# Feed-forward, first product: six 256-column products a block pair in two PSUM banks, instead of 512- and 256-column products in four

## The reference, cut to what matters

```
def squared_relu_mlp(h, w1, w2):
    return jnp.square(jax.nn.relu(h @ w1)) @ w2      # w1: 2048 x 8192, w2: 8192 x 2048

x = x + squared_relu_mlp(rms_norm(x, norm_ffn_g[l]), w_ff1[l], w_ff2[l])
```

## Time and profile before

| | us |
|---|---|
| median of 3 runs | 1606.09 (1605.94 to 1606.55) |
| span of the profiled execution | 1604.8 |
| TensorE busy in it | 1595.9 |
| VectorE busy | 1252.5 |
| ScalarE busy | 866.1 |
| FF1 of groups 1, 2, 3, each | 89.16, 89.17, 89.17 |
| FF2 of groups 1, 2 | 84.33, 84.97 |

### The profile page before, as it was taken

The page is one execution under the profiler, slowest core; times in us unless marked ns, Lnnn a source line. Parts: engine busy times, 40 slices in busy tenths (PEclk is TensorE's granted clock), DMA queues, the critical chain, the costliest instruction groups (busy, mean ns, idle before and its releaser), DMA issues.

```text
span 1604.8 us, 22691 instructions
## 1 busy us (share of the span) xinstructions
PE 1595.9 (99%) x7962; PEld 1352.9 (84%) x7962; DVE 1252.5 (78%) x1681; ACT 866.1 (54%) x1120; POOL 75.9 (5%) x160
## 2 busy tenths in 40 slices
PE   9999999999999999999999999999999999999998
PEld 8888888888888888888888888888888888888886
DVE  5588889999989898786887665885677666866587
ACT  7444456555555556754566655454464455545555
POOL 6500010000000000000000000000000000000001
PEclk9999999999999999999999999999999999999999
DMA  7665645555555665556664566666666666666555
GB/s 256 203 192 184 196 151 171 177 176 174 184 171 170 210 207 181 200 183 238 210 197 138 164 186 191 201 198 190 190 211 196 182 185 196 197 197 187 192 187 182
DMA packets 161294, 304.97 MB, mean 190 GB/s; under 512 B 11689, under 2 KB 20513, under 8 KB 160801
## 3 DMA queue, kind: packets, MB, share of 16 engines
q1 hardware_dynamic: 160128, 300.45, 58.9%
q0 software_dynamic: 1056, 3.46, 0.6%
q10 hardware_dynamic: 32, 0.01, 0.0%
HBM read 301.78 MB, written 2.10 MB: 189 GB/s over the span
## 4 chain that ended last, share of the span: by engine, by line
PE 98%; DVE 1%; DMA 1%; issue 0%; ACT 0%; SPq 0%; ACTq 0%; POOL 0%; DVEq 0%; POOLq 0%
PE ps L2255 15%; PE ps L1750 12%; PE ps L1752 12%; PE ps L1751 12%; PE ps L2025 9%; PE ps L2024 9%; PE ps L2023 9%; PE ps L2257 7%; PE ps L1763 1%; PE ps L1929 1%; PE ps L2146 1%; PE ps L1932 1%; PE ps L1914 1%; PE ps L1913 1%; PE ps L1912 1%; DMA raw<-in_w_ff_dram 1%
## 5 line engine op out<-in xcount | busy, mean ns | idle before, releaser
L1079 DVE TENSOR_TENSOR w_both<-raw,w_both 128x1024 fp32r<-128x1024 f32 x538 | 656.6, 1223 | 257.0 <-ACT w_both L624 255.3
L624 ACT ACTIVATE w_both<-raw 128x1024 fp32r<-128x1024 f32 x538 | 568.7, 1060 | 527.7 <-PE ps L1752 181.7
L2255 PE MATMUL ps<-a_both,w_both 128*128 128x512 f32 x1024 | 321.9, 396 | 0.0
L1750 PE MATMUL ps<-w_both,a_both 128*128 128x512 f32 x636 | 252.4, 397 | 0.1
L1752 PE MATMUL ps<-w_both,a_both 128*128 128x512 f32 x636 | 248.3, 390 | 0.0
L1751 PE MATMUL ps<-w_both,a_both 128*128 128x512 f32 x636 | 248.2, 390 | 0.0
L2257 PEld LDWEIGHTS ps<-a_both,w_both 128*128 128x128 f32 x1024 | 192.5, 188 | 45.2
L1140 DVE SCALAR_TENSOR_TENSOR acc<-hconv,cwk,acc 128x256 f32<-128x256 f32 x464 | 205.1, 497 | 7.4 <-PE ps L1968 7.4
L2257 PE MATMUL ps<-a_both,w_both 128*128 128x256 f32 x1024 | 201.4, 278 | 0.0
L2023 PE MATMUL ps<-w_both,c_hi 128*128 128x512 f32 x504 | 196.7, 390 | 0.3 <-DVE w_both L1079 0.3
L2025 PE MATMUL ps<-w_both,c_lo 128*128 128x512 f32 x504 | 196.4, 390 | 0.0
(11 more groups left out here) (377 smaller groups left out, 1920.3 us busy)
## 6 DMA issues: line engine op xcount, KB each, us to landing
raw<-in_w_ff_dram SPq DMA_DIRECT2D x256, 512.0 KB, 4.1
raw<-in_w_in_dram SPq DMA_DIRECT2D x144, 512.0 KB, 3.6
raw<-in_w_mla_out_dram SPq DMA_DIRECT2D x32, 512.0 KB, 3.7
raw<-in_w_conv_out_dram SPq DMA_DIRECT2D x32, 512.0 KB, 4.3
raw<-in_w_out_dram SPq DMA_DIRECT2D x32, 512.0 KB, 4.5
raw<-in_w_ukv_dram SPq DMA_DIRECT2D x16, 512.0 KB, 3.8
raw<-in_w_xkv_dram SPq DMA_DIRECT2D x16, 512.0 KB, 4.0
raw<-in_w_uq_dram SPq DMA_DIRECT2D x16, 384.0 KB, 3.3
```

What stands on the lines that cost most here:

```text
L624: act.activation(whi[:, s, :], raw[:, s, :], ACT.Copy).then_inc(hi_ready, 1)
L1079: dve.tensor_tensor(wlo[:, s, :], raw[:, s, :], whi[:, s, :].bitcast(F32), ALU.subtract).then_inc(lo_ready, 1)
L1750: pe.matmul(sum_, x_hi[:, k0 + k, tok], w_hi, start=(first and k == 0), stop=False)
L2255: pe.matmul(both, whi[:, s, cols[n]], a_both[:, :, k0 + k, :], start=(first and k == 0), stop=False)
```

## The change

In FF1 every bank now holds two blocks of 128 hidden columns, 256 tokens each, so that a chunk takes two banks (0 and 1, or 4 and 5) in place of four. A block's three products (`whi` x `a_hi`, `whi` x `a_lo`, `wlo` x `a_hi`), each of 256 columns, accumulate in the same columns. `ff_take` and `ff_add` are gone with `ff_low` and `ff_sum`; `ff_relus` reads the two banks directly and waits for `used` itself, and it now stands ahead of the `lo` of its step. TensorE waits for `ff_relu` where it waited for `ff_sum`.

```diff
         def ff1_banks(c):
-            return slice(CPB * (c % 2), CPB * (c % 2 + 1))
+            return slice(CPB * (c % 2), CPB * (c % 2) + 2)
...
-            def ff_take(n):
-                c = n % CH
-                act.activation(ff_row[:, c % 2, :, :], ps[:, ff1_banks(c), SEQ:], ACT.Copy).then_inc(ff_low, 1)
...
-                    act.wait_ge(used, r + (U_FF + UPC * (c + 1)))
-                    if c >= 2:
-                        act.wait_ge(ff_lo, g * CH + (c - 1))
-                    if c == 2:
-                        act.wait_ge(h_made, g * 4 + 12)
-                    ff_take(c)
...
-            def ff_add(c, done):
-                dve.wait_ge(ff_low, done)
-                row = ff_row[:, c % 2, :, :]
-                dve.tensor_tensor(row, ps[:, ff1_banks(c), 0:SEQ], row, ALU.add).then_inc(ff_sum, 1)
-            def ff_relus(c, done):
-                dve.wait_ge(ff_sum, done)
+            def ff_relus(c, units, done):
+                dve.wait_ge(used, units)
+                wait(dve, ff_lo, done - 2)
                 row = ff_row[:, c % 2, :, :]
+                sums = ps[:, ff1_banks(c), :].rearrange("p b (k s) -> p (b k) s", k=2)
                 by = rs_row[:].rearrange("p (k s) -> p k s", k=1).to_broadcast([P, CPB, SEQ])
-                dve.scalar_tensor_tensor(out=row, in0=row, scalar=0.0, in1=by, op0=ALU.max, op1=ALU.mult).then_inc(ff_relu, 1)
+                dve.scalar_tensor_tensor(out=row, in0=sums, scalar=0.0, in1=by, op0=ALU.max, op1=ALU.mult).then_inc(ff_relu, 1)
...
+                        if first and c == 1 and k == 0:
+                            dve.wait_ge(rs_row_ready, 1)
                         if c and k == 0:
-                            ff_add(c - 1, g * CH + c)
+                            ff_relus(c - 1, r + (U_FF + UPC * c), g * CH + c)
...
-                        if c and k == 0:
-                            ff_relus(c - 1, g * CH + c)
...
                 for k in range(2):
-                    for b in range(0, CPB, 2):
-                        cols = [slice(NC * k + P * n, NC * k + P * (n + 1)) for n in (b, b + 1)]
-                        for n in range(2):
-                            both = ps[:, b0 + b + n, :].rearrange("p (h s) -> p h s", h=2)
-                            pe.matmul(both, whi[:, s, cols[n]], a_both[:, :, k0 + k, :], start=(first and k == 0), stop=False)
-                        for n in range(2):
-                            mm = pe.matmul(ps[:, b0 + b + n, 0:SEQ], wlo[:, s, cols[n]], a_hi[:, k0 + k, :], start=False, stop=(last and k == 1))
+                    for half in range(2):
+                        blocks = [(ps[:, b0 + n, SEQ * half:SEQ * (half + 1)], slice(NC * k + P * (2 * n + half), NC * k + P * (2 * n + half + 1)))
+                                  for n in range(2)]
+                        for to, cols in blocks:
+                            pe.matmul(to, whi[:, s, cols], a_hi[:, k0 + k, :], start=(first and k == 0 and half == 0), stop=False, skip_group_check=True)
+                        for to, cols in blocks:
+                            pe.matmul(to, whi[:, s, cols], a_lo[:, k0 + k, :], start=False, stop=False, skip_group_check=True)
+                        for to, cols in blocks:
+                            mm = pe.matmul(to, wlo[:, s, cols], a_hi[:, k0 + k, :], start=False, stop=(last and k == 1 and half == 1), skip_group_check=True)
```

More of the change, by code:

```diff
@@ L383, in build @@
         rs_spread, rs_turned, rs_row_ready = (sem(n) for n in ("rs_spread", "rs_turned", "rs_row_ready"))
-        ff_low, ff_sum, ff_relu, ff_square, ff_hi, ff_lo = (sem(n) for n in ("ff_low", "ff_sum", "ff_relu", "ff_square", "ff_hi", "ff_lo"))
+        ff_relu, ff_square, ff_hi, ff_lo = (sem(n) for n in ("ff_relu", "ff_square", "ff_hi", "ff_lo"))
         h_lifted, h_made, h_hi_ready, h_lo_ready = (sem(n) for n in ("h_lifted", "h_made", "h_hi_ready", "h_lo_ready"))
@@ L1665, in ff_group @@
                             last_diag.then_inc(rs_spread, 1)
-                        if first and c == 1 and k == 0:
-                            dve.wait_ge(rs_row_ready, 1)
-                        if c and k == 0:
-                            ff_relus(c - 1, g * CH + c)
                         if c and k == 2:
@@ L1677, in ff_group @@
                         if p == 0 and k == 0:
-                            ff_add(CH - 1, g * CH + CH)
+                            ff_relus(CH - 1, r + (U_FF + UPC * CH), g * CH + CH)
                         i = k + LEAD
@@ L1685, in ff_group @@
                             lo(U_FF + u + i, r)
-                        if p == 0 and k == 0:
-                            ff_relus(CH - 1, g * CH + CH)
                         if p == 0 and k == 3:
@@ L2268, in ff_group @@
                     else:
-                        pe.wait_ge(ff_sum, g * CH + (c - 1))
+                        pe.wait_ge(ff_relu, g * CH + (c - 1))
                     for k in range(UPC):
@@ L2281, in ff_group @@
                             mm.then_inc(rs_turned, 1)
-                pe.wait_ge(ff_sum, g * CH + (CH - 1))
+                pe.wait_ge(ff_relu, g * CH + (CH - 1))
                 def ff_waits(i, k):
@@ L2286, in ff_waits @@
                     if i == LEFT[0]:
-                        pe.wait_ge(ff_sum, g * CH + CH)
+                        pe.wait_ge(ff_relu, g * CH + CH)
                 def mixed_waits(i, k):
```

## The result

| | before | after |
|---|---|---|
| median of 4 runs, us | 1606.01 (1605.94 to 1606.55) | 1618.54 (1618.43 to 1619.33) |
| ratio, 95% interval | | 1.0078 [1.0065, 1.0090] |
| span of the profiled execution | 1604.8 | 1616.7 |
| TensorE busy, products | 1595.9, 7962 | 1608.1, 8986 |
| VectorE, ScalarE busy | 1252.5, 866.1 | 1236.4, 851.9 |

What follows compares the result with a forecast made beforehand. The prediction took TensorE's products to bound the kernel: +12.0 for FF1's short products, +0.1 backlog and -0.6 for the gap gave +11.5 us, so 1606.1 + 11.5 = 1617.6 us, range 1606 to 1620.

Steps and rivals of the forecast that it cites:

- TensorE is the path, the rest lies beside it: Whole kernel: TensorE, busy 1595.9 of 1604.8 us, sets the end; ScalarE and VectorE work counts only where TensorE waits.
- A round costs 0.720 us for 0.6966, +12.0 us: FF1: six 256-column products at 0.120 us replace a round of four; 512 rounds at +0.0234 us each give +12.0 us.
- Rival 3: FF1: supplying 768 products unbroken costs another 1 to 2 ns each, 1621 to 1624 us; chance 0.05, shared with another rival.
- The reason given for it: FF1: the 128-column weight load, no longer hidden under a 512-column neighbour, sets an unbroken train's pace at 120 ns.
- the sign would turn: FF1: at 116.1 ns a product (696.6 / 6) the change would turn from slower to faster.
- The page's rule: FF1: the skill's load of 107 ns for 128 columns hides under a 256-column product; round 680 ns, sum -8.5 us.
- rival 1: FF1: loads hide under 256-column products and the round falls to 680 ns, -8.5 - 0.6, 1597.0 us; chance 0.08.
- The backlog: End of each FF1 stretch: two or three products late by 5 to 10 ns, 0.1 us in all.
- The ramp from PSUM: Behind each FF1 chunk: the ramp takes 1.22 to 1.23 us from PSUM, `lo` ends a microsecond earlier; cost nothing.
- The busy times forecast: Copy and add removed from FF1: 16.5 us less busy on ScalarE, 19.7 on VectorE; DVE near 1233, ACT near 850.
- The gap: FF2: 0.60 us lost behind two late transfers; everything from the first `lo` on comes 1.0 us earlier, so -0.6 us.
- The sum: Whole kernel: +12.0 + 0.1 - 0.6 = +11.5 us, span 1616.3, median 1617.6 us.

Runs made afterwards that it cites:

- e_no_add: Kernel before with its own products but no copy and add; the ramp leaves the high-weights, low-tokens product out of the sum: 1606.31 us, ratio 1.0000.
- e_tok240: Changed kernel with 240 of 256 tokens moving in FF1's products, all 128 weight columns loaded: 1593.62 us.
- e_tok128: Changed kernel with 128 of 256 tokens moving in FF1, all 128 weight columns loaded: 1593.36 us; the same with 224 tokens: 1592.80 us.
- e_cols64: Changed kernel with only 64 of each block's 128 weight columns loaded in FF1, 256 tokens still moving: 1602.35 us.
- e_tok192: Changed kernel with 192 of 256 tokens moving in FF1, all 128 weight columns loaded: 1593.15 us.
- e_alternate: Kernel before with an FF1 round's products by turns, 512, 256, 512, 256 columns in place of 512, 512, 256, 256: 1609.78 us, ratio 1.0022.
- e_fours: Kernel before with two FF1 rounds drawn together, four products of 512 columns, then four of 256: 1608.69 us, ratio 1.0015.
- e_cols96: Changed kernel with 96 of each block's 128 weight columns loaded in FF1, 256 tokens still moving: 1606.31 us.

## Why the prediction was right, point by point

- **TensorE is the path, the rest lies beside it.** Right. After the change no wait of TensorE behind the kernel's start is left in the list of waits, and without the element work alone the time stays where it was (e_no_add: 1606.31 beside 1606.22).
- **A round costs 0.720 us for 0.6966, +12.0 us.** Right: 92.16 a stretch was forecast and measured. The number came from rows of the same shape, not from a price for a load and one for columns. That is what made it hold. Rival 3, the supply of the train, fell: 768 products in a row keep the pace of 36, and e_tok240 sends as many 0.1117 apart, so the supply doesn't set 0.120.
- **The reason given for it** (the 128-column load sets the pace at 120 ns) was only half right. The floor that I take for the load's pace is 111.6 ns (e_tok128, 192, 224, 240) and the columns alone 113.3 (e_cols64 in groups 1 to 3); 120 is what the two give together. Both lie under 116.1, the point where the sign would turn, so a sum from separate prices would have said faster. The sentence that misled is "The forms differ in the weight load, which takes 192 ns for 128 columns and 135 for 64": a length in a row is no pace (192 ns loads start 111.6 apart in e_tok192). Nor was it safe to read from the key that a 64-column load gives 113.3: e_cols64 holds 120 with such loads for 600 products. And more than the load differs between the two rows, the moving operand too. The runs bear out that the load's size counts in FF1; the two rows alone did not show it.
- **The page's rule.** The Trainium skill gives 107 ns for such a load ("TensorE: Matmul & The Clock Gate", "LDWEIGHTS (loading the stationary operand)"), near the floor of 111.6 measured here. What the case contradicts is the step from there to "hidden": rival 1 would have come at 1597.0.
- **The backlog, +0.1 us.** Too small to see: the FF2 stretches behind a train are 84.34, before 84.33.
- **The ramp from PSUM costs nothing.** Right. The timeline of TensorE and VectorE behind the first chunk's end (926.63), answering to the earlier trace rows:

```profile
926.39 0.40 PE L2240 MATMUL ps<-a_both,w_both 128*128 128x256 f32 x2
926.63 0.40 PE L2236 MATMUL ps<-a_both,w_both 128*128 128x256 f32 x2
...
926.90 1.23 DVE L1625 SCALAR_TENSOR_TENSOR ff_row<-ps,rs_row 128x1024 f32<-128x1024 f32 x1 [1.02 <-PE ps L2240]
928.05 1.22 DVE L1068 TENSOR_TENSOR w_both<-raw,w_both 128x1024 fp32r<-128x1024 f32 x1
```

  The ramp takes 1.23 us; the `lo` ends at 929.27, 2.6 us behind the chunk's end, where it was 3.6 and 2.7 was forecast. The busy times forecast were too low: VectorE lost 16.1 us and not 19.7, ScalarE 14.2 and not 16.5. Rows overlap (the add's 1.23 us start 1.15 ahead of the next row), so a removed row takes less than its length off the busy time. Nothing on the path hangs on it.
- **The gap goes, -0.6 us.** It went (84.97 to 84.34), but the reason given isn't borne out, and here the forecast had luck. The copy and the add gone, the chain a microsecond earlier, a gap of 0.48 us stayed in e_no_add, with a transfer of 6.60 us in its chain as one of 6.72 in the earlier trace rows. And with the copy and the add still there it was gone in e_alternate (and in e_fours, 84.37). That the slower FF1 gives the transfers more time doesn't explain it either: in e_cols96 FF1 takes 89.1 as before, in e_cols64 87.05, and there is no gap (e_tok128, at 85.7, has a small one, 84.60). FF2 of group 2 in e_cols96, then in e_alternate:

```profile
1339.67:1424.01 84.34, 84.34 (x375) 69.80 (x373) 67.41 (x63) 43.34 (x46) 0.00 (x0) 1.00 0.62 206
1341.85:1426.19 84.34, 84.34 (x374) 69.85 (x373) 68.45 (x64) 44.26 (x47) 0.00 (x0) 1.00 0.63 205
```

  Each trace is one execution. A transfer that happens to be late in one and not in another would fit all of these (the prediction's own "a slow transfer can fall elsewhere"); it isn't shown.
- **The sum.** +11.5 forecast on the span, +11.9 found: 12.0 less 0.63, and 0.48 from the part ahead of FF1, which is as large as the spread of the runs there. The median came at +12.5. The +12.0 is the part that was understood; that the small terms left the total within 1 us of 1617.6 is partly luck.

## What to carry to other kernels

When products fill the engine, count how they sit in their train and not only their columns: 512-column products ran at 0.4428 ns a column, 256-column ones with full weight loads at 0.469, mixed rounds between 0.452 and 0.460, by their order and by where they stood in the kernel. Work taken off engines that nobody waits for (31 us in e_no_add) buys nothing, so it is no payment for shorter products on the one that all wait for. Price a new form by the nearest whole train in the trace, start to start, and distrust a sum of single prices.

## What the runs showed of the hardware that was not expected

- **A third pace.** In an unbroken train with 128 weight columns a product starts every 111.6 or 111.7 ns for 128, 192, 224 and 240 moving columns, and every 120.0 ns for 256. Sixteen more columns cost 8.3 ns, where sixteen columns at the long products' pace are 7.1 and 240 of them would fit in 106.3. At 256 columns the loads of 64, 96 and 128 columns give 113.3 (in one stretch 120), 116.0 and 120.0.
- **The same instructions, two steady paces in one execution.** e_cols64 runs 600 products at 120 ns in group 0 and 768 at 113.3 in each group after; e_alternate 0.6942 us a round in group 0 and 0.7066 after. In e_cols64 the pace changes inside group 0, from 113.3 to 120 ns, at the four 128-column products L2263; behind eight transposes of 128 columns (908.03) it did not, and behind the FF2 stretches it is 113.3 again. In e_alternate the same four products change nothing (0.693 us a round from 914.09 to 922.41, 0.6942 after), and the slower pace comes behind FF2. With 128 weight columns FF1 of the kernel after shows 120 in all groups, on both sides of the four products. What stands ahead of a train seems to set its pace; no run set it on purpose, and the mechanism stays open.
- **Mixed rounds are not a sum.** Neither a fixed price for each load under a short product nor a backlog that long products work off predicts the ranking of groups 1 to 3, by turns (slowest), four and four, two and two; and in group 0 by turns is the fastest of the three.
